# A new order for ScalarE's weight blocks and for VectorE's norm work in the MLP of a hybrid decoder step

## What is computed

```python
u, gv = jnp.split(rmsnorm(h, p["norm_ffn_g"]) @ p["w_up"], 2, axis=-1)
u, new_ffn_buf = causal_dwconv(u, ffn_buf, p["ffn_conv_w"])
h = h + (jax.nn.silu(u) * gv) @ p["w_down"]
```

## Time and profile before

| | |
|---|---|
| timed runs, median of 3 | 2013.07 us (2009.49 to 2013.34) |
| profiled execution | 2004.87 us |
| its span in the trace | 2003.1 us |
| mean granted TensorE clock | 0.982 |
| MLP steps in the trace | 1181 us to the end |
| one steady step (step 2's stall to step 3's) | 71.46 us |

### The profile page before, as it was taken

The page is one execution under the profiler, slowest core; times in us unless marked ns, Lnnn a source line. Parts: engine busy times, 40 slices in busy tenths (PEclk is TensorE's granted clock), DMA queues, the critical chain, the costliest instruction groups (busy, mean ns, idle before and its releaser), DMA issues. The chain is left out here.

```text
span 2003.1 us, 33089 instructions
## 1 busy us (share of the span) xinstructions
PE 1833.5 (92%) x13009; PEld 1721.7 (86%) x13009; DVE 1126.2 (56%) x1480; ACT 637.9 (32%) x1186; POOL 726.6 (36%) x599
## 2 busy tenths in 40 slices
PE   6988999999998999999998798899999999999997
PEld 6966899977877788999987688898889889889897
DVE  6877277745443233462244497665565665656566
ACT  6056336722332005320134453222222231222223
POOL 3411133412112135646752044433433443343344
PEclk9999999999999999999999998899999999999999
DMA  4311111111002031323223110101101111110122
GB/s 186 91 38 44 39 44 38 46 52 37 27 26 79 17 117 60 132 84 109 67 74 134 64 36 32 57 29 42 63 21 63 42 42 42 42 53 31 42 67 87
DMA packets 45487, 119.75 MB, mean 60 GB/s; under 512 B 3808, under 2 KB 20768, under 8 KB 44224
## 3 DMA queue, kind: packets, MB, share of 16 engines
q1 hardware_dynamic: 45392, 118.39, 17.9%
HBM read 102.95 MB, written 15.77 MB: 59 GB/s over the span
## 5 line engine op out<-in xcount | busy, mean ns | idle before, releaser
L628 PE MATMUL PS<-XH,WH 128*128 128x352 f32 x1224 | 407.9, 333 | 36.1 <-POOL WL L858 14.0
L628 PE MATMUL PS<-XH,WL 128*128 128x352 f32 x1224 | 395.1, 323 | 0.0
L628 PE MATMUL PS<-XL,WH 128*128 128x352 f32 x1224 | 394.9, 323 | 0.0
L904 POOL TENSOR_TENSOR WL<-RAW,WH 128x512 fp32r<-128x512 f32 x176 | 249.8, 1431 | 289.9 <-ACT WH L1396 289.8
L628 PEld LDWEIGHTS PS<-XH,WH 128*128 128x128 f32 x1224 | 231.7, 189 | 50.4 <-issue 32.8
L628 PEld LDWEIGHTS PS<-XL,WH 128*128 128x128 f32 x1224 | 232.1, 190 | 3.9 <-issue 3.4
L866 POOL TENSOR_TENSOR WH<-RAW,CST 128x256 fp32r<-128x256 f32 x90 | 64.0, 738 | 463.6 <-PE PS L1607 193.4
L628 PEld LDWEIGHTS PS<-XH,WL 128*128 128x128 f32 x1224 | 231.7, 189 | 0.0
L1396 ACT ACTIVATE WH<-RAW 128x512 fp32r<-128x512 f32 x176 | 107.2, 627 | 312.9 <-PE PS L2227 155.6
L2276 PE MATMUL PS<-XH,WH 128*128 128x352 f32 x396 | 137.3, 347 | 54.7 <-POOL WL L904 53.8
L2998 DVE TENSOR_TENSOR TMP<-TMP,PS 128x352 f32<-128x352 f32 x154 | 78.0, 520 | 183.9 <-PE PS L2276 181.9
(11 more groups left out here) (510 smaller groups left out, 4229.2 us busy)
## 6 DMA issues: line engine op xcount, KB each, us to landing
RAW<-in_w SPq DMA_DIRECT2D x136, 512.0 KB, 3.5
H<-in_xT SPq DMA_DIRECT2D x4, 1056.0 KB, 9.1
TMP<-in_xT SPq DMA_DIRECT2D x2, 2112.0 KB, 8.5
early_gates<-DV SPq DMA_DIRECT2D x18, 176.0 KB, 2.0
out_yT<-H SPq DMA_DIRECT2D x4, 704.0 KB
early_gates<-A SPq DMA_DIRECT2D x12, 176.0 KB, 1.8
DV<-early_gates SPq DMA_DIRECT2D x1, 2112.0 KB, 14.1
TMP<-early_gates SPq DMA_DIRECT2D x2, 1056.0 KB, 5.4
```

The lines of the kernel that those rows point to most:

```text
L628: mm = nc.tensor.matmul(PS[:, 3 * mm_g + c, 0:CW], w_[:, p, off + k * P:off + (k + 1) * P], x_[:, xk0 + k, c * CW:(c + 1) * CW], start=fir ...
L904: nc.gpsimd.tensor_tensor(WLB[:, i % 4, :], src, WHB[:, i % 4, :].bitcast(F32), ALU.subtract).then_inc(w_split, 1)
```

## The change

ScalarE's order in a step: head 3 of the gate pair comes before `mlp_u(f, 1)`, head 4 before the first Silu, and heads 5 to 7 before the second; the Silus become a function, `mlp_silu`. TensorE's norm sum in step 0 moves behind the product `p7`. VectorE's list ahead of step 0 puts `t3`'s difference and rests before the last two additions of squares. The scalings `unnormed`: four stood after the second convolution of step 0 and four at its end; now scaling 0 stands after the convolution, 1 and 2 after `combine` 2 and 8 of the gate pair, 3 in step 1 before `combine` 1, 4 after `combine` 2 of the up pair, 5 and 6 after `combine` 2 and 7 after `combine` 8 of its gate pair. VectorE's step 1 is written out, and its loop starts at 2.

```diff
@@ -1460,6 +1460,11 @@
                 nc.scalar.activation(f_tail[:, t, 0:2], x[:, TP:TP + 2], ACT.Copy).then_inc(fp_ok, 1)
                 nc.scalar.activation(f_tail[:, t, 2:18].rearrange("p (b n) -> p b n", b=NB), new[:, :, 2:4], ACT.Copy).then_inc(fp_ok, 1)
 
+            def mlp_silu(f, i):
+
+                act.wait_ge(f_cv, 12 * f + 6 * i + 6)
+                nc.scalar.activation(f_act[:, i, :], f_act[:, i, :], ACT.Silu).then_inc(f_silu, 1)
+
             def gated_heads(f, out):
                 for i in range(2):
                     nc.scalar.activation(out[:, i, :], f_act[:, i, :], ACT.Copy).then_inc(f_hi, 1)
@@ -1490,16 +1495,15 @@
                 pair_head(f, 1, 0)
                 pair_head(f, 1, 1)
                 pair_head(f, 1, 2)
+                pair_head(f, 1, 3)
                 mlp_u(f, 1)
-                pair_head(f, 1, 3)
                 copy_p1(f, 1)
-                for i in range(2):
-                    act.wait_ge(f_cv, 12 * f + 6 * i + 6)
-                    nc.scalar.activation(f_act[:, i, :], f_act[:, i, :], ACT.Silu).then_inc(f_silu, 1)
                 pair_head(f, 1, 4)
+                mlp_silu(f, 0)
                 pair_head(f, 1, 5)
                 pair_head(f, 1, 6)
                 pair_head(f, 1, 7)
+                mlp_silu(f, 1)
                 if not first:
                     for i in range(4):
                         down_head(f, i)
@@ -2317,13 +2321,13 @@
                 pe.wait_ge(w_split, SLOTS["ffn"][0] + b + 5)
                 pe.wait_ge(f_copied, n_copy + 1)
                 product(bank["p5"], 0, "t1", first).then_inc(w_used, 1)
-                if first:
-                    pe.wait_ge(xo_free, 8)
-                    norm_sum(pe, 3)
                 pe.wait_ge(w_split, SLOTS["ffn"][0] + b + 6)
                 if g == 0:
                     pe.wait_ge(f_ev, n_ev + 1)
                 product(bank["p7"], 1, "t3", first).then_inc(w_used, 1)
+                if first:
+                    pe.wait_ge(xo_free, 8)
+                    norm_sum(pe, 3)
                 pe.wait_ge(w_split, SLOTS["ffn"][0] + b + 7)
                 pe.wait_ge(f_ev, n_ev + 3 if g == 0 else n_ev - 11 + 10)
                 last_third(bank["x1"], 2, 0, False).then_inc(w_used, 1)
@@ -2955,12 +2959,12 @@
             weight_s3(0, 0)
             x_rest_of("x11", 2)
             x_rest_of("x11", 3)
+            x_difference("t3", 3)
+            x_rest_of("t3", 2)
+            x_rest_of("t3", 3)
             norm_add(dve, 3, 6, T)
             norm_add(dve, 3, 7, T)
-            x_difference("t3", 3)
             x_difference("t4", 3)
-            x_rest_of("t3", 2)
-            x_rest_of("t3", 3)
             x_rest_of("t4", 2)
             x_rest_of("t4", 3)
 
@@ -3068,13 +3072,18 @@
 
             def mlp_dve(f):
                 zero = isinstance(f, int) and f == 0
+                one = isinstance(f, int) and f == 1
                 last = isinstance(f, int) and f == FT // 2 - 1
                 if not zero:
                     rests(f - 1, AH, AL)
+                if one:
+                    unnormed(3)
                 for i in range(1, 9):
                     if zero and i == 7:
                         dve.wait_ge(nrs, 4)
                     combine(f, 0, i)
+                    if one and i == 2:
+                        unnormed(4)
                 mlp_conv(f, 0)
                 weight_s1(f, 1)
                 weight_s2(f, 1)
@@ -3085,19 +3094,24 @@
                 mlp_conv(f, 1)
                 if zero:
                     dve.wait_ge(nrs, 5)
-                    for k in range(4):
-                        unnormed(k)
+                    unnormed(0)
                 for i in range(1, 12):
                     combine(f, 1, i)
+                    if zero and i in (2, 8):
+                        unnormed(1 + i // 8)
+                    if one and i == 2:
+                        unnormed(5)
+                        unnormed(6)
+                    if one and i == 8:
+                        unnormed(7)
                 if zero:
                     weight_s1(1, 0)
                     weight_s2(1, 0)
                     weight_s4(1, 0)
                     weight_s3(1, 0)
-                    for k in range(4, 8):
-                        unnormed(k)
+                    return
+                if one:
                     dve.wait_ge(f_z, 9)
-                    return
                 for m in range(KT):
                     down_sum(f - 1, m)
                     if m == 1 and last:
@@ -3109,7 +3123,8 @@
                         weight_s4(f + 1, 0)
                         weight_s3(f + 1, 0)
             mlp_dve(0)
-            with dve.Fori(1, FT // 2 - 1) as f:
+            mlp_dve(1)
+            with dve.Fori(2, FT // 2 - 1) as f:
                 mlp_dve(f)
             mlp_dve(FT // 2 - 1)
 
```

## The result

| | before | after |
|---|---|---|
| timed runs, median | 2013.2 us (2009.49 to 2015.87, 4 runs) | 1945.68 us (1940.97 to 1949.25, 4 runs) |
| profiled execution | 2004.87 us | 1944.93 us |
| its span | 2003.1 us | 1943.1 us |
| mean granted clock | 0.982 | 0.989 |
| a steady step, down start to down start | 71.5 to 71.9 us | 65.1 to 65.7 us |

The ratio after to before is 0.9664, with a 95% interval of 0.9638 to 0.9691: faster by 3.4%. The profiled execution lost 59.9 us.

What follows compares the result with a forecast made beforehand. TensorE, busy 92%, was taken as the bound, stalling each step for GpSimd's late `WL`. 54.9 + 6.9 - 2.8 = 59.0 us off 2004.87 gave 1945.9 profiled, 1954 for the median; range 1940 to 1968, extended to 1978.

Steps and rivals of the forecast that it cites:

- Items 1 and 2: Steps 2 to 10: ScalarE's new order removes 6.6 us a step, a new 0.5 us wait comes; 54.9 us gained.
- A turn: Second convolution: each of GpSimd's rests 4 to 7 delays VectorE by 1.15 us, 4.6 us in all.
- Item 3: Step 1: VectorE's moved scalings remove one wait and add one before the down product; 6.9 us gained, bounds 3 and 12.
- Item 4: Step 0: the later norm sum delays VectorE's chain and step 1's start; -2.8 us in all, bounds 0 and -6.
- Item 5: VectorE's step 1 written out instead of looped: same operations, costed at nothing.
- GpSimd held off by the convolution: Steps 2 to 10: rest 5 waits until VectorE's convolution ends; only 28 us gained, 1985 us; chance 13%.
- VectorE's chain later: Every step: one more turn of 1.15 us before `combine` 7 or the second Silu; 48 us gained, 1965; chance 11%.
- The order doesn't get ahead: ScalarE: head 4 is held by its slot or `copy_p1`, so only the first two steps change; 2012 us; chance 2%.
- The clock: Steps 2 to 10: TensorE without stalls is granted less clock; at 0.88 the time is 2032 us; chance 2%.
- The first step costs 10 us more: Step 0 costs 10 us more than forecast, still 1964 us; chance 2%.

Runs made afterwards that it cites:

- the repeat: The kernel before with only ScalarE's new order, run a second time with nothing else altered: 1938.97 us, ratio 0.9644.
- the kernel with one head late: The kernel after with the second Silu put back before head 7: 1967.8 us in one run.

## Why the prediction was right, step by step

The profiled execution was forecast at 1945.9 us and measured 1944.93; the forecast 1954 for the median was 8 us high only because the kernel before's profiled execution lay 8 us below its own median, and this one's doesn't (1944.93 and 1945.68). The saving from the profile, 59.0, met 59.9, but that it came so close is luck. Counted from the common event the parts gained 56.3 + 8.6 - 2.3 = 62.6 us, every one of them more than forecast, and 2.65 of that went to the event, which came so much later in this execution in code that the change doesn't touch.

- **Items 1 and 2, steps 2 to 10: right.** Forecast 54.9 us; from step 1's down product to the end it was 1296.89 to 2003.1 before and is 1293.20 to 1943.1 after: 706.2 less 649.9, 56.3. Head 4 comes right behind `copy_p1`, the rests run during the convolution, and each takes a turn. Two terms of the sum were off, and nearly cancel. A turn costs 0.97 us (the convolution is 3.9 us longer, for four rests), not 1.15, so VectorE is early and the 0.5 us wait before the down product isn't there: `combine` 7 ends at 1423.90, TensorE is ready at 1424.41. And the products' pace is 0.160 us, not 0.1586 (65.3 over 408): I had taken the pace from one stretch, where the kernel before shows 0.1595 over all. A step of 64.7 plus 0.5 and one of 65.3 with nothing are nearly the same.
- **Item 3, step 1: forecast 6.9 us, measured 8.6.** From its first product to its down product it took 54.5 us before and takes 47.5, which is 7.0 less although it holds the slow start of 1.6 that item 4 had counted. The wait of 4.05 us at the third-from-last product is gone, as worked out (the sum has 4.2 for it, the row 4.05). The new one before the down product is 2.96 us instead of 4.0, and the granted clock after it is 1.00, where I had put 1.5 us for a slow restart. There is luck in that: neither execution of this kernel had slow products there, but behind the same wait two other kernels had some, worth 1.6 and 2.8 us (above):

```profile
1293.20:1297.20 4.00, 4.00 (x25) 4.00 (x26) 3.96 (x5) 0.00 (x0) 1.14 (x1) 1.00 0.68 228
```

- **Item 4, the first step: forecast -2.8 us, measured -2.3** (56.8 less 56.1, and 12 products in 3.47 us instead of 1.9). Less the 2.65 us of that execution, `combine` 7 starts at 1212.5 (forecast 1211.9) and step 1's first product at 1243.1 (forecast 1243.6), after 5.62 us of idling (forecast 6). Ln's table load ran at 1205.21, before the wait. `t3` started 0.5 us later than I had it, behind a hole of 5.42, and then 12 products at 0.29 us, both forecast. Not foreseen was a wait of 1.26 us for gate block 0 (1218.71); it is absorbed, since VectorE sets the start of step 1.
- **Item 5: nothing to see**, as said.
- **The rivals.** *GpSimd held off by the convolution* fell: no rest in the convolution took over 2.3 us (the last of the three in 5.24), under the 2.5 that I had named, and they came in turn. But its mechanism exists, 4.09 us during four scalings in two executions and 4.27 ahead of the event in all, and the repeat shows that the same instructions can also alternate. The argument that a rest already queued gets its turn was borne out in every convolution and was never tested by itself. *VectorE's chain later* fell in steps 2 to 10, by 0.5 us of slack. *The order doesn't get ahead* fell. *The clock* fell: 1.00 in a step without a gap. *The first step costs 10 us more* fell: 0.7 us, as the whole of steps 0 and 1 gained 6.3.
- What the prediction left out: it took the change as a whole. It gave steps 0 and 1 a gain of 4.1 us (6.9 less 2.8), and they gained 6.3, but with ScalarE's order alone they gain 12.5 (110.7 less 98.2). So the norm sum's and the scalings' new places, which the sum credits with removing waits, cost some 6 us beside what the new order brings by itself. With the norm sum back the distance is 100.6 us instead of 104.3 and 105.5, so 4 to 5 of the 6 are the norm sum's; the rest was not taken apart. The medians of the timed runs go the same way: 1940.41 and 1938.97 against 1945.68 and 1944.44.

The rule of the Trainium skill (SBUF — State Buffer, "SBUF: two separate sides"), that the later one of the two engines blocks for the other's whole instruction, holds in the convolution: 1.61 and 2.37 us for operations of 0.75 and 1.29. For a rest that comes into VectorE's operations issued back to back it held in one execution of ScalarE's order alone (1.77 us, a wait for the rest of one scaling) and not in the other (4.09 us, a wait for all that were left of four). There the measurement decides: the later engine can block for longer than one instruction.

## What to carry to other kernels

Ahead of an instruction that waits long, look in the same queue for work behind it that is ready and that another engine wants: here four copies behind one Silu were worth 3.5%. A move that fills a hole elsewhere has to be tried by itself, above all when what is moved feeds a chain that sets the end: the norm sum ran in a hole for nothing, and moved behind a product that was itself waiting it delayed what came after it by 4 to 5 us. Work without a due time, such as the scalings, is best put where its engine would next wait for TensorE anyway. Of the two placements tried here, the one that spread them over step 0's gate pair and both pairs of step 1 came out 7 us behind the one that kept step 0 free of them and put four beside the down product.

## What the runs showed that I had not expected

- GpSimd and VectorE, both with operands in SBUF, took turns in the second convolution of every step, where VectorE's operations wait for one another and GpSimd's rests are mostly already queued (0.97 us to VectorE for each rest). Which of the two conditions decides was not tried. Into a run of independent operations of VectorE GpSimd got in some executions only after all of them (4.09 and 4.28 us instead of 1.27), and in one, with the same program, after the first.
- The slow products after a wait need not begin with the first. In the kernel with one head late, TensorE starts again at 1558.85, after a wait of 1.88 us, with a product of 0.43 us and one at full speed, and only then 12 go slowly. The stretch has a granted clock of 0.59:

```profile
1558.85:1563.00 4.15, 4.15 (x16) 4.15 (x17) 2.42 (x4) 0.41 (x1) 3.07 (x2) 0.59 0.40 126
```

  The same wait one step earlier, at 1491.23, had none of it, nor had the 2.96 us at 1293.20, where 2.93 us at the same place in the kernel with the norm sum back had 20 slow products. So the first product's 0.43 us, which the prediction took as a sign of full speed, is none; the granted clock of the next 4 us is. A wait of 1.9 to 3 us can't be priced closer than 0 to 2.8 us more, and what decides stays open.
- The kernels' times differ in code that is the same in all: the event at 1186.24 came between 1186.2 and 1191.9 in the executions here, and steps of the same kernel differ by 0.6 us. A few microseconds of a difference between two traces are no effect until counted from an event that both share.
